# A two-block transformer kernel: the feed-forward up and gate products streamed as 512 columns into a whole PSUM bank

## The chip, the core and the metric

One core of a Trainium2 chip runs the whole program as one launch. The engines of a core are TensorE (PE; its weight loads are listed as PEld), VectorE (DVE), ScalarE (ACT), GpSimd (POOL) and SyncE (SP, which here only issues loads of weights). Matrix products accumulate in PSUM, which has eight banks of 512 fp32 columns on 128 partitions. The metric is the device time of the kernel in microseconds (us), as the median of several runs; less is better.

## The reference

The input is 256 rows (tokens) of 1024 numbers. Two transformer blocks follow one another. What matters here are their three feed-forward parts, one in the first block and two in the second:

```
# first block
a, v = split(h @ w_up)                    # h = rmsnorm(x), 1024 -> 2 x 2816
a    = causal depthwise conv, 3 taps, + bias
x    = x + (gelu(a) * v) @ w_down         # 2816 -> 1024
# second block, before and after its attention
x    = x + 0.5 * ((silu(h @ w_gate) * (h @ w_up)) @ w_down)
```

All inputs and outputs are fp32, and each product is computed to about fp32 accuracy.

## The kernel before

**Products.** TensorE reads fp32 here in a faster, rounded format (F32R). So every operand is split into a high half (the rounded value, made by ACT) and a low half (the rest, made by DVE), and a product is three matmuls: high x high, high x low, low x high, added up in PSUM. The helper `three` (line 336) does it for each block of 128 contracted numbers.

**Units.** Weights come in 158 units, nearly all of 1 MB, in the order of a plan. For unit i, SP loads `raw[i % 3]`, ACT copies it to `wh[i % 3]` (line 880), DVE subtracts and writes `wl[i % 3]` (line 1292). `hi_to(i)` and `lo_to(i)` make the halves up to unit i; `begin(key, ahead=2)` makes them up to two units past `key`. ACT's copy waits until the products of unit i - 3 are done, SP's load until `wl` of unit i - 3 is made. Each engine runs its own program strictly in the order in which it is written; semaphores tie them together.

**A feed-forward part** `ffn(f, k, ...)` (f = 0, 1, 2; k numbers the norm ahead of it) runs over 11 steps j. Step j has two up units, ("up", f, j, 0), here called the a unit, and ("up", f, j, 1), the v unit. Each gives 256 columns of the inner width, turned so that they lie on partitions (two groups m of 128), for 256 tokens: 2 groups x 8 blocks k x 3 matmuls of 256 tokens, 48 matmuls, into one bank (`rows_out`). Then comes the down unit of step j - 1 with 24 matmuls of 512 columns, whose sums stay in banks 2 to 5. The turned rows of h stand in `hTh` and `hTl`, 256 columns for each block. DVE takes a unit out of its bank and multiplies by `RB`, the norm's factor for each token (`rows_scaled`, line 1376). ACT applies silu (for f = 0: three taps, ACT's on line 1165, DVE's on line 1842, and gelu on line 1168), DVE multiplies a and v (line 1851), ACT and DVE split the result into `yTh` (line 1182) and `yTl` (line 1862), and only then does each of them make its halves of one more weight unit.

**The start of a part.** Step j = 0 runs its two units as a pair (`norm_pair`), in four stretches of 24 matmuls: blocks 4 to 7 of a, then of v, then blocks 0 to 3 of a, then of v, because blocks 0 to 3 of h come last. Eight transposes (line 385) stand after the first stretch and a small product (line 399), which spreads the token factors, after the third. A pair takes four banks, one for each unit and group m, and its factors are applied by `pair_scaled` (line 1367). At this place ACT makes `wh` of the two units that follow the pair.

**Banks.** Up units take turns on banks 0, 1, 6, 7 (`WF`); the projections ahead of a part use banks 0 and 1 (`W`); transposes and spreads use 2 to 5. A unit's first matmul waits until the engine that emptied the bank before has counted it free (`take`).

Of the kernel before, what the change touches and what calls it, by code (L numbers as in the profile page):

```python
# [123 lines left out]
def build(nc, plan, I, out):  # L124
    ctx = ExitStack()
    with ctx:
# [9 lines left out]
        wl = [sb(f"wl{i}", 2048, F32R) for i in range(NS)]  # L136
        hTh, hTl = sb("hTh", 2048, F32R), sb("hTl", 2048, F32R)
        X, Hn = sb("X", 2048), sb("Hn", 2048)
# [13 lines left out]
        F2 = sb("F2", 256)  # L152
        bank = [ctx.enter_context(nc.psum_tensor(f"ps{i}", [128, 512], F32)) for i in range(8)]

# [48 lines left out]
        mrg_fox, mrg_all, m_hi, m_lo = (sem(n) for n in ("mrg_fox", "mrg_all", "m_hi", "m_lo"))  # L203

        cv_in, cv_out, ff_act, ff_y, y_hi, y_lo = (sem(n) for n in ("cv_in", "cv_out", "ff_act", "ff_y", "y_hi", "y_lo"))

# [71 lines left out]
        def hT_at(k):  # L278
            return hTh[:, k * 256:k * 256 + 256], hTl[:, k * 256:k * 256 + 256]

        def yT_at(k):
            return yTh[:, k * 256:k * 256 + 256], yTl[:, k * 256:k * 256 + 256]
# [34 lines left out]
        def pe_program(pe):  # L317
            W, T = Banks(0, 1), Banks(2, 3, 4, 5)
            WF = Banks(0, 1, 6, 7)

# [9 lines left out]
            def three(o, lw, rw, ks, first, last, ready=None):  # L330
                (lh, ll), (rh, rl) = lw, rw
                for k in ks:
                    for j, (l, r) in enumerate(((lh, rh), (lh, rl), (ll, rh))):
                        if j == 0 and ready is not None and (k == ks[0] or k % 2 == 0):
                            pe.wait_ge(*ready(k))
                        ins = pe.matmul(o, l(k), r(k), start=first and k == ks[0] and j == 0,  # L336
                                        stop=last and k == ks[-1] and j == 2)
                return ins

# [14 lines left out]
            def rows_out(key, banks, mid=None):  # L354
# [3 lines left out]
                for m in range(2):  # L358
                    ins = three(t[:, m * 256:m * 256 + 256], weight_left(i, 256, m * 128), right(hT_at),
                                EIGHT, True, True)  # L360
                    if m == 0 and mid:
                        mid()
                ins.then_inc(ps_full[b], 1)
                unit_end[i] = full(key)
# [38 lines left out]
            def norm_pair(key0, key1, k):  # L403
                keys = (key0, key1)
                bs = [[WF.take(), WF.take()] for _ in range(2)]
                for half, ks in enumerate(((4, 5, 6, 7), (0, 1, 2, 3))):
                    for j in range(2):
# [13 lines left out]
                        if half:  # L421
                            unit_end[i] = full(keys[j] + (1,))
                        if half and j == 0:
                            spread(k)
# [323 lines left out]
            def ffn(f, k, k_next):  # L748
                for j in range(11):
                    if j == 0:  # L750
                        norm_pair(("up", f, 0, 0), ("up", f, 0, 1), k)
                    else:
                        rows_out(("up", f, j, 0), WF)
                        rows_out(("up", f, j, 1), WF)
                    if 1 <= j < (9 if k_next is None else 10):
# [23 lines left out]
            def last_units(f):  # L779
# [14 lines left out]
                unit_end[U["down", f, 9]] = full(("acc", f, 1))  # L794

                for h in range(2):
                    b = WF.take()
                    t = take(("last", h), b)
# [4 lines left out]


            norm_pair(("qa", 0), ("ka", 0), 3)
            toks_out(("va", 0), W)
# [61 lines left out]
        def act_program(act):  # L868
# [49 lines left out]
            def norm_turns(k, hold):  # L918
                act.wait_ge(*x_ready(k, 0))
                act.wait_ge(*x_ready(k, 1))  # L920
                squares(k, 0)
                if hold is not None:
                    act.wait_ge(*unit_end[hold])
                for p in (0, 1):
# [220 lines left out]
            def toeplitz():  # L1145
# [136 lines left out]
        def dve_program(dve):  # L1282
# [537 lines left out]
            def ffn(f, k, scale, k_next):  # L1820
                for j in range(11):
# [4 lines left out]
                    if j == 0:  # L1826
                        norm_pair(ka, k)
                        pair_scaled(g, ka)
                        pair_scaled(gv, kv)
                        lo_to(U[ka] + 3)  # L1830
                    else:
                        begin(ka)
                        rows_scaled(g[:, :], ka)
                        begin(kv)
# [11 lines left out]
                    if j:  # L1846
                        rows_scaled(gv[:, :], kv)
                        dve.wait_ge(*free(kv))
                    else:
                        dve.wait_ge(*free(kv + (1,)))  # L1850
                    dve.tensor_tensor(g[:, :], gv[:, :], c[:, :], ALU.mult).then_inc(ff_y, 1)  # L1851
# [377 lines left out]
```

## Time and profile before

| what | value |
|---|---|
| median of 3 runs | 1000.81 us (1000.48 to 1001.31) |
| profiled execution, its own time | 1000.7 us |
| span of its trace | 998.9 us |
| PE busy | 985.7 us, 99% |
| weight loads busy | 944.4 us, 95% |
| DVE busy | 665.8 us, 67% |
| ACT busy | 487.1 us, 49% |
| POOL busy | 69.0 us, 7% |
| weights and inputs read | 172.21 MB, 173 GB/s over the span |

A busy time is the union of an engine's instructions. Matmuls overlap one another: a record of one is 0.28 us long, but one starts every 0.12 us. So what a matmul costs is read from the distance between starts, or from a long piece of the chain divided by its count, and not from its own duration. For DVE and ACT the duration is nearly the cost; the next independent instruction starts 0.05 to 0.1 us before the end of the one ahead.

### The profile page before, as it was taken

What the parts mean: (1) busy time and instruction counts of PE and PEld (TensorE: products, weight loads), DVE (VectorE), ACT (ScalarE), POOL (GpSimd) and SP (SyncE); (2) the same over time, 40 slices, a digit from 0 to 9 for tenths busy, and PEclk for the clock granted to TensorE, in tenths of its full rate; (3) what the DMA queues carried; (4) which work ended last, traced back from release to release, by engine and by line L of the source; (5) the groups of instructions that cost most, each with busy time, mean ns of one, the idle gap of its engine ahead of it and who ended that gap; (6) DMA issues with size and microseconds to landing.
All of it is one profiled execution on the core that took longest, in us unless ns stands there. A gap on an engine that the chain in (4) does not pass through costs nothing.

```text
span 998.9 us, 17282 instructions
## 1 busy us (share of the span) xinstructions
PE 985.7 (99%) x7438; PEld 944.4 (95%) x7438; DVE 665.8 (67%) x849; ACT 487.1 (49%) x588; POOL 69.0 (7%) x148
## 2 busy tenths in 40 slices
PE   7999999999999999999999999999999999999997
PEld 7999999999999999999899999999999999999996
DVE  5679767775776766676675555557777576555565
ACT  6654656565355545444554333336545453333343
POOL 0010123234210000000000000000002000000000
PEclk9999999999999999999999999999999999999999
DMA  9744444343455555454456455553533445555541
GB/s 337 279 133 163 135 161 170 132 152 140 138 206 210 211 189 191 172 200 156 174 185 208 172 183 197 171 192 134 179 131 123 142 174 212 183 197 171 192 144 43
DMA packets 26539, 174.37 MB, mean 175 GB/s; under 512 B 3424, under 2 KB 3808, under 8 KB 6368
## 3 DMA queue, kind: packets, MB, share of 16 engines
q1 hardware_dynamic: 25744, 170.23, 48.0%
q10 hardware_dynamic: 720, 3.04, 0.8%
q8 instruction: 59, 0.97, 0.4%
q14 instruction: 16, 0.13, 0.0%
HBM read 172.21 MB, written 1.05 MB: 173 GB/s over the span
## 4 chain that ended last, share of the span: by engine, by line
PE 98%; DVE 0%; ACT 0%; DMA 0%; issue 0%; ACTq 0%
PE ps L336 90%; PE ps L570 2%; PE ps L621 2%; PE ps L385 1%; PE ps L489 1%; PE ps L584 1%; DMA GT<-in_gains 0%; PE ps L399 0%; PE ps L479 0%; PE ps L514 0%; DVE hTl L1321 0%; ACT hTh L894 0%; ACT hTh L916 0%; PE ps L513 0%; PE ps L497 0%
## 5 line engine op out<-in xcount | busy, mean ns | idle before, releaser
L336 PE MATMUL ps<-hTh,wh 128*128 128x256 f32 x1512 | 432.4, 286 | 6.8 <-DVE wl L1407 6.5
L336 PE MATMUL ps<-hTh,wl 128*128 128x256 f32 x1512 | 428.7, 284 | 0.0
L336 PE MATMUL ps<-hTl,wh 128*128 128x256 f32 x1512 | 428.6, 283 | 0.0
L1292 DVE TENSOR_TENSOR wl<-raw,wh 128x2048 fp32r<-128x2048 f32 x153 | 350.7, 2293 | 109.4 <-ACT wh L880 109.3
L880 ACT ACTIVATE wh<-raw 128x2048 fp32r<-128x2048 f32 x156 | 295.6, 1899 | 177.3 <-PE ps L336 173.1
L336 PEld LDWEIGHTS ps<-hTh,wh 128*128 128x128 f32 x1512 | 290.1, 192 | 9.5 <-DVE wl L1407 6.5
L336 PEld LDWEIGHTS ps<-hTl,wh 128*128 128x128 f32 x1512 | 290.0, 192 | 1.4
L336 PEld LDWEIGHTS ps<-hTh,wl 128*128 128x128 f32 x1512 | 290.0, 192 | 0.2
L336 PE MATMUL ps<-wh,yTh 128*128 128x512 f32 (+1 forms) x330 | 123.3, 374 | 0.0
L336 PE MATMUL ps<-wl,yTh 128*128 128x512 f32 (+1 forms) x330 | 122.9, 373 | 0.0
L336 PE MATMUL ps<-wh,yTl 128*128 128x512 f32 (+1 forms) x330 | 122.8, 372 | 0.0
L336 PE MATMUL ps<-wh,hTh 128*128 128x256 f32 x384 | 110.8, 289 | 0.0
L336 PE MATMUL ps<-wh,hTl 128*128 128x256 f32 x384 | 108.5, 283 | 0.0
L336 PE MATMUL ps<-wl,hTh 128*128 128x256 f32 x384 | 108.5, 283 | 0.0
L1376 DVE TENSOR_TENSOR PT<-ps,RB 128x512 f32<-128x512 f32 x60 | 41.4, 691 | 74.2 <-PE ps L336 67.2
L1182 ACT ACTIVATE yTh<-PT 128x512 fp32r<-128x512 f32 x33 | 20.9, 634 | 110.9 <-DVE PT L1851 107.1
L336 PEld LDWEIGHTS ps<-wl,hTh 128*128 128x128 f32 x384 | 73.6, 192 | 0.1
L336 PEld LDWEIGHTS ps<-wh,hTh 128*128 128x128 f32 x384 | 73.4, 191 | 0.1
L336 PEld LDWEIGHTS ps<-wh,hTl 128*128 128x128 f32 x384 | 73.5, 191 | 0.0
L336 PEld LDWEIGHTS ps<-wh,yTl 128*128 128x128 f32 x330 | 62.1, 188 | 11.9
L336 PEld LDWEIGHTS ps<-wh,yTh 128*128 128x128 f32 x330 | 62.3, 189 | 10.6
L336 PEld LDWEIGHTS ps<-wl,yTh 128*128 128x128 f32 x330 | 62.2, 188 | 10.6
(250 smaller groups left out, 791.6 us busy)
## 6 DMA issues: line engine op xcount, KB each, us to landing
raw<-in_units SPq DMA_DIRECT2D x155, 1024.0 KB, 4.9
BIGT<-in_bias ACTq DMA_DIRECT2D x1, 2048.0 KB, 7.5
XT<-in_x_turned SPq DMA_DIRECT2D x4, 256.0 KB, 5.4
raw<-in_units SPq DMA_DIRECT2D x4, 256.0 KB, 5.6
raw<-in_units SPq DMA_DIRECT2D x2, 512.0 KB, 8.2
X<-in_x SPq DMA_DIRECT2D x1, 1024.0 KB, 8.5
Hn<-in_mem SPq DMA_DIRECT2D x1, 1024.0 KB, 10.0
XT<-in_mem_turned SPq DMA_DIRECT2D x1, 1024.0 KB, 12.1
```

The source lines that it names most:

```text
L336: ins = pe.matmul(o, l(k), r(k), start=first and k == ks[0] and j == 0, stop=last and k == ks[-1] and j == 2)
L385: ins = pe.transpose(t[:, q * 128:q * 128 + 128], src[:, m * n + k * 128:m * n + k * 128 + 128], ident)
L489: ins = pe.matmul(t[:, q * 128:q * 128 + 128], s, s, start=True, stop=True)
L570: ins = pe.matmul(t[:, x:z], l, r, start=True, stop=True)
L584: ins = pe.transpose(t[:, j * 128:j * 128 + 128], src[:, o:o + 128], ident)
L621: ins = pe.matmul(at_o(m), turned(a, i)[:, j * 128:j * 128 + 128], at_v(kb), start=x == 0, stop=x == len(js) - 1)
L880: act.activation(wh[j % NS][:, 0:n], raw[j % NR][:, 0:n], ACT.Copy).then_inc(w_hi, 1)
L1182: act.activation(yTh[:, j % 2 * 512:j % 2 * 512 + 512], g[:, :], ACT.Copy).then_inc(y_hi, 1)
L1292: dve.tensor_tensor(wl[j % NS][:, 0:n], raw[j % NR][:, 0:n], wh[j % NS][:, 0:n].bitcast(F32), ALU.subtract).then_inc(w_lo, 1)
L1376: ins = dve.tensor_tensor(o, i, by_token(2), ALU.mult)
```

## The change

The two halves of h become one tensor `hT`, with `hTh` and `hTl` as its two parts, and the eight banks become one tensor `ps`. For the up units alone, a new helper `crossed` runs two matmuls instead of three for each block and group: the high weights against both halves of h at once (512 columns, read as two pieces of 256 which lie 2048 columns apart), then the low weights against the high half (256 columns, added to the second half of the bank). A unit then fills two whole banks, one for each group m, and the result is the sum of a bank's two halves. ACT copies the second halves out of PSUM into `Am` (`second_sums`), DVE adds them to the first halves (`up_scaled`, first instruction) and then multiplies by `RB` (second instruction). Up units take turns on two pairs of banks, (0, 1) and (6, 7). The counters of `W` and `WF` are set back to zero after the second part.

```diff
+        def hT_both(k):
+            return hT[:, :].rearrange("p (s n) -> p s n", s=2)[:, :, k * 256:k * 256 + 256]
...
+            def crossed(o, lw, ks, first, last, ready=None):
+                lh, ll = lw
+                for k in ks:
...
+                    pe.matmul(o, lh(k), hT_both(k), start=first and k == ks[0], stop=False)
+                    ins = pe.matmul(o[:, 256:512], ll(k), hT_at(k)[0], start=False, stop=last and k == ks[-1])
+                return ins
...
-            WF = Banks(0, 1, 6, 7)
+            WF, UP = Banks(0, 1, 6, 7), Banks(0, 6)
...
+            def take_two(key):
+                b = UP.take()
+                return b, [take(key, b), take(key + ("x",), b + 1, False)]
...
# ACT
+            def second_sums(key):
+                n, (_, t) = up_no(key), sums(key)
+                act.wait_ge(*full(key))
+                if n >= 2:
+                    act.wait_ge(*free(up_key(n - 2)))
+                act.activation(v3(crossed_out(n)), t, ACT.Copy).then_inc(cross_made, 1)
...
                     if j == 0:
-                        norm_pair(keys[0], k)
+                        hi_to(U[keys[0]] + 1)
+                        norm_turns(k, U["wo", k, 1] if k == 1 or k == 4 else U["up", k - 2, 10, 1])
+                        second_sums(keys[0])
+                        hi_to(U[keys[0]] + 3)
                     else:
                         begin(keys[0])
+                        second_sums(keys[0])
                         begin(keys[1])
-                    act.wait_ge(*free(keys[0] if j else keys[0] + (1,)))
+                    act.wait_ge(*scaled(keys[0]))
...
+                    if not j:
+                        second_sums(keys[1])
...
+                    if j:
+                        second_sums(keys[1])
...
# DVE
+            def up_scaled(dst, key):
+                n, d, (t, _) = up_no(key), v3(dst), sums(key)
+                dve.wait_ge(cross_made, n + 1)
+                dve.tensor_tensor(d, t, v3(crossed_out(n)), ALU.add).then_inc(*emptied(key))
+                dve.wait_ge(*free(key))
+                dve.tensor_tensor(d, d, by_token(2), ALU.mult).then_inc(*emptied(key + ("x",)))
...
-                        pair_scaled(g, ka)
-                        pair_scaled(gv, kv)
+                        up_scaled(g[:, :], ka)
+                        up_scaled(gv[:, :], kv)
                         lo_to(U[ka] + 3)
...
+            W.n, WF.n = 0, 0
             norm_pair(("qa", 0), ("ka", 0), 3)
```

How the programs stand at three places follows. Names in the rows: `ps_full` counts filled banks, `ps_free` emptied ones, the digit is the bank.

ACT at the start of the second part, before, from the last block of h (`hTh`) on: the two copies `wh` are those of the a and v units of step 1.

```order
L894 ACTIVATE hTh<-ps4,GT 128x256 [waits ps_full4,ps_full0]
L894 ACTIVATE hTh<-ps4,GT 128x256
L894 ACTIVATE hTh<-ps5,GT 128x256 [waits ps_full5]
L894 ACTIVATE hTh<-ps5,GT 128x256
L880 ACTIVATE wh0<-raw0 128x2048 [waits raw_in0,ps_full5]
L880 ACTIVATE wh1<-raw1 128x2048 [waits raw_in1,ps_full6]
L1174 ACT_TABLE_LOAD
L1174 ACTIVATE P0<-PT0 128x512 [waits ps_free6]
```

The same place with the change:

```order
L963 ACTIVATE hT<-ps,GT 128x256
L963 ACTIVATE hT<-ps,GT 128x256 [waits ps_full5]
L963 ACTIVATE hT<-ps,GT 128x256
L1225 ACTIVATE Am<-ps 128x512 [waits ps_free0,ps_full0]
L949 ACTIVATE wh0<-raw0 128x2048 [waits raw_in0,ps_full5]
L949 ACTIVATE wh1<-raw1 128x2048 [waits raw_in1,ps_full0]
L1225 ACTIVATE Am<-ps 128x512 [waits ps_free6,ps_full6,ps_free1]
L1256 ACT_TABLE_LOAD
L1256 ACTIVATE P0<-PT0 128x512
```

A copy out of PSUM that waits for the a unit of the pair (`ps_full0`) now stands ahead of both `wh` copies; before, only the second of them waited for that unit.

PE at the start of the first part, before: the last matmuls of the projection's last unit, which fills bank 0, and the first two of the pair.

```order
L336 MATMUL ps<-wh,hTh 128x256
L336 MATMUL ps<-wl,hTh 128x256
L336 MATMUL ps<-wh,hTl 128x256
L336 MATMUL ps<-hTh,wh 128x256 [waits ps_free3,w_lo,ps_free1]
L336 MATMUL ps<-hTl,wh 128x256
```

The same place with the change, where the projection's last unit fills bank 0 as well:

```order
L360 MATMUL ps<-wh,hT 128x256 x2
L360 MATMUL ps<-wl,hT 128x256
L360 MATMUL ps<-wh,hT 128x256
L370 MATMUL ps<-hT,wh 128x512 [waits w_lo,ps_free3,ps_free1,ps_free0]
L371 MATMUL ps<-hT,wl 128x256
```

The pair's first matmul waited for bank 1; it now waits for banks 0 and 1, and bank 0 is the one that the unit just ahead of it has filled. At the start of the third part the last projection fills bank 1, and it is bank 1 that is new in the wait. 
PE at the start of the first part, before: the end of the pair and the first matmuls of the unit after it.

```order
L336 MATMUL ps<-hTh,wh 128x256
L336 MATMUL ps<-hTl,wh 128x256
L336 MATMUL ps<-hTh,wl 128x256
L336 MATMUL ps<-hTh,wh 128x256 [waits w_lo,ps_free1]
L336 MATMUL ps<-hTl,wh 128x256
```

The same place with the change:

```order
L370 MATMUL ps<-hT,wh 128x512
L371 MATMUL ps<-hT,wl 128x256
L370 MATMUL ps<-hT,wh 128x512 [waits w_lo,ps_free1,ps_free0]
L371 MATMUL ps<-hT,wl 128x256
L370 MATMUL ps<-hT,wh 128x512
```

The unit after a pair now waits for two banks. Bank 0 counts as free after DVE's addition for the pair's a unit, bank 1 after the multiplication behind it. Before, this matmul waited for one bank alone, which one instruction of `pair_scaled` empties.

## Rows read from the trace of the kernel before

**Rows 1.** The page: busy time by engine, and the chain by engine and line.

```profile
PE 985.7 (99%) x7438; PEld 944.4 (95%) x7438; DVE 665.8 (67%) x849; ACT 487.1 (49%) x588; POOL 69.0 (7%) x148
PE 98%; DVE 0%; ACT 0%; DMA 0%; issue 0%; ACTq 0%
```

**Rows 2.** The chain in order of time: start, length, work, count.

```profile
497.84 5.75 PE ps L336 x48
...
769.05 1.29 PE ps L621 x12
...
813.01 179.76 PE ps L336 x1254
```

**Rows 3.** PE in order of time: start, length of record. First part, the pair's first matmul.

```profile
303.01 0.28 PE L336 MATMUL ps<-hTh,wh 128*128 128x256 f32 x1
```

**Rows 4.** DVE in order of time: the addition that empties the projection's last bank.

```profile
303.21 0.69 DVE L1810 TENSOR_TENSOR X<-X,ps 128x512 f32<-128x512 f32 x1 [0.38 <-PE ps L336]
```

**Rows 5.** DVE, then PE: a wait of PE that ends, second part's start.

```profile
492.83 1.66 DVE L1321 SCALAR_TENSOR_TENSOR hTl<-ps,GT,hTh 128x256 fp32r<-128x256 f32 x4 [0.35 <-ACT hTh L894]
493.86 0.35 PE L336 MATMUL ps<-hTh,wh 128*128 128x256 f32 x1 [0.15 <-DVE hTl L1321]
```

**Rows 6.** ACT in order of time, second part's start; then a PSUM copy elsewhere.

```profile
498.94 1.93 ACT L880 ACTIVATE wh<-raw 128x2048 fp32r<-128x2048 f32 x1
503.63 1.92 ACT L880 ACTIVATE wh<-raw 128x2048 fp32r<-128x2048 f32 x1 [2.76 <-PE ps L336]
...
140.54 0.60 ACT L1024 ACTIVATE P<-ps 128x512 f32<-128x512 f32 x1 [1.19 <-PE ps L514]
141.03 1.91 ACT L880 ACTIVATE wh<-raw 128x2048 fp32r<-128x2048 f32 x1
```

**Rows 7.** DVE in order of time, second part's start.

```profile
502.50 2.28 DVE L1292 TENSOR_TENSOR wl<-raw,wh 128x2048 fp32r<-128x2048 f32 x1
504.70 0.42 DVE L1351 COPY RB<-ps 128x256 f32<-128x256 f32 x1
505.15 0.76 DVE L1367 TENSOR_TENSOR PT<-ps,RB 128x256 f32<-128x256 f32 x2
```

**Rows 8.** PE in order of time: the first matmul of the unit after the pair.

```profile
506.75 0.28 PE L336 MATMUL ps<-hTh,wh 128*128 128x256 f32 x1
```

**Rows 9.** ACT in order of time, first part, step 1.

```profile
331.40 0.63 ACT L1168 ACTIVATE P<-P 128x512 f32<-128x512 f32 x1 [2.81 <-DVE P L1842]
333.52 0.63 ACT L1182 ACTIVATE yTh<-PT 128x512 fp32r<-128x512 f32 x1 [1.48 <-DVE PT L1851]
334.05 3.70 ACT L880 ACTIVATE wh<-raw 128x2048 fp32r<-128x2048 f32 x2
```

**Rows 10.** DVE in order of time, first part, step 1.

```profile
326.79 0.68 DVE L1376 TENSOR_TENSOR PT<-ps,RB 128x512 f32<-128x512 f32 x1
327.39 2.28 DVE L1292 TENSOR_TENSOR wl<-raw,wh 128x2048 fp32r<-128x2048 f32 x1
329.58 1.78 DVE L1842 SCALAR_TENSOR_TENSOR P<-PT,VT,P 128x255 f32<-128x255 f32 x4
332.07 0.69 DVE L1376 TENSOR_TENSOR PT<-ps,RB 128x512 f32<-128x512 f32 x1 [0.70 <-ACT P L1168]
332.79 0.69 DVE L1851 TENSOR_TENSOR PT<-PT,P 128x512 f32<-128x512 f32 x1
335.99 4.49 DVE L1292 TENSOR_TENSOR wl<-raw,wh 128x2048 fp32r<-128x2048 f32 x2 [1.11 <-ACT wh L880]
```

**Rows 11.** Stretches: start:end, their length, PE, PEld, DVE, ACT, POOL busy, PEclk.

```profile
6.50:11.70 5.20, 5.19 (x24) 5.19 (x25) 3.99 (x9) 4.39 (x9) 0.00 (x0) 1.00 0.98 347
992.00:993.00 1.00, 0.76 (x7) 0.55 (x5) 0.70 (x3) 0.38 (x2) 0.00 (x0) 1.00 0.99 371
994.50:995.00 0.50, 0.00 (x0) 0.00 (x0) 0.43 (x3) 0.07 (x1) 0.00 (x0) 0.77 0.00 0
995.00:995.50 0.50, 0.00 (x0) 0.00 (x0) 0.50 (x1) 0.50 (x1) 0.00 (x0) 0.50 0.00 0
```

More of the change, by code:

```diff
@@ L136, in build @@
         wl = [sb(f"wl{i}", 2048, F32R) for i in range(NS)]
-        hTh, hTl = sb("hTh", 2048, F32R), sb("hTl", 2048, F32R)
+        hT = sb("hT", 4096, F32R)
+        hTh, hTl = hT[:, 0:2048], hT[:, 2048:4096]
         X, Hn = sb("X", 2048), sb("Hn", 2048)
@@ L152, in build @@
         F2 = sb("F2", 256)
-        bank = [ctx.enter_context(nc.psum_tensor(f"ps{i}", [128, 512], F32)) for i in range(8)]
+        ps = ctx.enter_context(nc.psum_tensor("ps", [128, 4096], F32))
+        bank = [ps[:, 512 * i:512 * i + 512] for i in range(8)]
         used = [0]
@@ L279, in hT_at, with sums, scaled, up_no @@
             return hTh[:, k * 256:k * 256 + 256], hTl[:, k * 256:k * 256 + 256]
+        def hT_both(k):
+            return hT[:, :].rearrange("p (s n) -> p s n", s=2)[:, :, k * 256:k * 256 + 256]
+        def sums(key):
+            t = ps[:, 512 * at[key][0]:512 * at[key][0] + 1024].rearrange("p (m s n) -> p m s n", m=2, s=2)
+            return t[:, :, 0, :], t[:, :, 1, :]
+        def scaled(key):
+            return free(key + ("x",))
+        def up_no(key):
+            return 22 * key[1] + 2 * key[2] + key[3]
+        def up_key(n):
+            return "up", n // 22, n // 2 % 11, n % 2
+        def crossed_out(n):
+            return Am[:, n % 2 * 512:n % 2 * 512 + 512]
         def yT_at(k):
@@ L337, in three @@
                                         stop=last and k == ks[-1] and j == 2)
+                return ins
+            def crossed(o, lw, ks, first, last, ready=None):
+                lh, ll = lw
+                for k in ks:
+                    if ready is not None and (k == ks[0] or k % 2 == 0):
+                        pe.wait_ge(*ready(k))
+                    pe.matmul(o, lh(k), hT_both(k), start=first and k == ks[0], stop=False)
+                    ins = pe.matmul(o[:, 256:512], ll(k), hT_at(k)[0], start=False, stop=last and k == ks[-1])
                 return ins
@@ L362, in rows_out, with up_out @@
                         mid()
+                ins.then_inc(ps_full[b], 1)
+                unit_end[i] = full(key)
+            def take_two(key):
+                b = UP.take()
+                return b, [take(key, b), take(key + ("x",), b + 1, False)]
+            def up_out(key):
+                i = U[key]
+                b, ts = take_two(key)
+                weights(i)
+                for m in range(2):
+                    ins = crossed(ts[m], weight_left(i, 256, m * 128), EIGHT, True, True)
                 ins.then_inc(ps_full[b], 1)
@@ L422, in norm_pair, with up_pair @@
                             unit_end[i] = full(keys[j] + (1,))
+                        if half and j == 0:
+                            spread(k)
+            def up_pair(key0, key1, k):
+                keys, bs, ts = (key0, key1), [0, 0], [None, None]
+                for half, ks in enumerate(((4, 5, 6, 7), (0, 1, 2, 3))):
+                    for j in range(2):
+                        i = U[keys[j]]
+                        if not half:
+                            bs[j], ts[j] = take_two(keys[j])
+                            weights(i)
+                        for m in range(2):
+                            ins = crossed(ts[j][m], weight_left(i, 256, m * 128), ks, half == 0, half == 1,
+                                          (lambda k2: free(("n", k, k2 // 2))) if j == 0 and m == 0 else None)
+                        if half:
+                            ins.then_inc(ps_full[bs[j]], 1)
+                            unit_end[i] = full(keys[j])
+                        if not half and j == 0:
+                            norm_turn(k, 0)
+                            norm_turn(k, 1)
                         if half and j == 0:
@@ L750, in ffn @@
                     if j == 0:
-                        norm_pair(("up", f, 0, 0), ("up", f, 0, 1), k)
+                        up_pair(("up", f, 0, 0), ("up", f, 0, 1), k)
                     else:
-                        rows_out(("up", f, j, 0), WF)
-                        rows_out(("up", f, j, 1), WF)
+                        up_out(("up", f, j, 0))
+                        up_out(("up", f, j, 1))
                     if 1 <= j < (9 if k_next is None else 10):
@@ L794, in last_units @@
                 unit_end[U["down", f, 9]] = full(("acc", f, 1))
+                b0 = UP.take()
                 for h in range(2):
-                    b = WF.take()
+                    b = b0 + h
                     t = take(("last", h), b)
@@ L1832, in ffn @@
                         begin(ka)
-                        rows_scaled(g[:, :], ka)
+                        up_scaled(g[:, :], ka)
                         begin(kv)
@@ L1846, in ffn @@
                     if j:
[L1847 to L1850, printed above, removed]
+                        up_scaled(gv[:, :], kv)
+                    dve.wait_ge(*scaled(kv))
                     dve.tensor_tensor(g[:, :], gv[:, :], c[:, :], ALU.mult).then_inc(ff_y, 1)
```

4 lines of the change are left out of this document (2 added, 2 removed).

## The prediction

> **What bounds the kernel now.** I read the page first: PE is busy 99% of the span, and 98% of the chain that ended last is PE work [rows 1]. The chain in order of time then shows the feed-forward parts as single pieces, 1254 matmuls in 179.76 us in the third one, with no wait inside [rows 2]. So each ns of a matmul counts in full, and so does each ns that PE waits; DVE (67%) and ACT (49%) [rows 1] have room, on average. What they add costs nothing in the middle of a part unless a chain of their steps gets longer than PE's step, and it may cost at once where PE waits for their latest result. That place is the start of each part, so I read all engines there in order of time [rows 3 to 8].
>
> **What a matmul costs.** 48 matmuls of 256 columns take 5.75 us, 119.8 ns each [rows 2]. Of the 1254 in the third part, 996 have 256 columns; they leave 179.76 - 996 x 0.1198 = 60.4 us for 258 matmuls of 512, 234.3 ns each. Three of 256 cost 359.4 ns, one of 512 and one of 256 cost 354.1 ns: the same 768 columns pass, and only one start is saved. **The gain is 5.3 ns** for each block and group, 0.085 us a unit. There are 66 units x 16 = 1056 of them: **-5.6 us** in all.
> Bounds: if a 256 costs half a 512 (117.1 ns) once it stands behind one, the gain is 8.0 ns or 8.4 us. On the other side, no row shows an operand read as two pieces 2048 columns apart; if the second piece costs as much as a new start, the 512 costs 2 x 119.8 and the gain is nil. I take 5.3 ns, since the streamed columns are the same kind of F32R data as in both rows.
> The Trainium skill (TensorE: Matmul & The Clock Gate, Back-to-back issue gap) gives N/2.4 + 2.5 ns at the full clock, which would make one saved start worth 2.5 ns, an estimate of 2.6 us for the change. The rows are above it at both widths.
>
> **A new wait ahead of the first and the third pair.** The pair's first matmul starts at 303.01 [rows 3], right behind the projection's last unit. DVE empties that unit's bank from 303.21 to 303.90 [rows 4]. The pair will now ask for that bank. When a wait of PE ends, its matmul starts 0.14 us behind the releasing work (DVE's first two of four pieces end near 493.72, PE starts at 493.86), and its record is 0.07 us longer [rows 5]. So it starts at 303.90 + 0.14 + 0.07 = 304.11: 1.1 us late, twice, **+2.2 us**. The second part comes behind units that use other banks and doesn't pay.
>
> **A new wait behind each pair.** Second part, with times of before. ACT copied the high half of the unit behind the pair (P2) at 498.94, long before it was needed, and that of P3 at 503.63, when the pair's a unit was done [rows 6]. Now a copy out of PSUM that waits for the a unit stands ahead of both.
> - The a unit is done after three stretches, 0.04 us sooner each: 503.50. The PSUM copy holds ACT 0.49 us (140.54 to 141.03) [rows 6]. P2's high half starts at 503.99.
> - DVE subtracts 1.94 us later (334.05 to 335.99) [rows 9, 10]: at 505.93, instead of 502.50 [rows 7].
> - DVE's next steps keep their distances: `RB` 2.20 later at 508.13, the addition 0.45 later at 508.58 [rows 7], the multiplication, which needs its result, 0.72 later at 509.30 (332.07 to 332.79), done after 0.69 at 509.99 [rows 10].
> - P2 needs both banks of the a unit. It starts at 509.99 + 0.21 = 510.20. It started at 506.75 [rows 8], and with four shorter stretches would at 506.58. **The wait is 3.6 us**: DVE's work on the bank begins 3.4 us later (508.58 for 505.15 [rows 7]), and takes 1.4 us for both banks where one piece of some 0.4 was enough; 0.8 us of room is used up.
> Three parts: **+10.9 us**. The spread and the low half of the pair's factors have no part in it; they were ready at 502.50.
>
> **The first part has two more.** There the three taps make DVE's and ACT's chain longer. Let M be the end of the multiplication above; P2 starts at M + 0.2, P3 at M + 5.9, the first down unit should at M + 11.5. The chain: PSUM copy for v and its addition (M + 0.65), multiplication (+0.72), low half of P3 (+0.60), taps (+2.20), gelu (+1.82), a x v (+0.67), `yTh` (+0.73), high half of the down unit (+0.53), its low half (+1.94) for 2.29 us [rows 9, 10]: ends at M + 12.15, and PE goes on at M + 12.4. **+0.8 us.**
> One step on: additions from M + 12.06, low half 13.4, taps 15.6, gelu 17.4, then in turn PSUM copy, addition, multiplication, a x v, `yTh`, high half, 5.8 us together, and the low half of the next v unit from M + 23.2 to 25.5. PE, coming from M + 12.4 + 5.6 + 5.7 = M + 23.7, goes on at M + 25.7. **+2.1 us.** After that the chain's round (three low halves 6.6, addition and multiplication 1.3, taps 1.8, gelu 0.5, PSUM copy 0.6, addition to `yTh` 2.9, high half 1.9) is 15.6 us, 16.6 where ACT also turns a bias (1.05 us), against PE's 32 x 0.354 + 24 x 0.234 = 17.0. It catches up slowly. At the part's end the same chain from the last a unit is 11.2 us against PE's 11.3, which with the restart is worth **+0.2**. In the other parts there are no taps (2 us less), and nothing of this waits.
>
> **The sum.** -5.6 + 2.2 + 10.9 + 0.8 + 2.1 + 0.2 = +10.6 us, on the profiled execution's own 1000.7 us (span 998.9 and 1.8 around it; the median is 1000.81): 1011.3.
>
> **The clock.** PE was busy 99% [rows 1] and after its start the chain holds no wait as long as these. At the end PE's last work ends at 992.76, and the granted clock falls to half (1.2 GHz) near 994.77 (0.77 over that half us), 2.0 us later [rows 11]. A wait of 3.6 us is longer. At the kernel's start 24 matmuls took 5.19 us, where 24 x 0.12 = 2.9 is full speed [rows 11, 2], though the record there reads 1.00; that is half speed (1.2 GHz) after idling: 2.3 us is the most that one fall costs, nothing the least. I take the middle, 1.1, since the fall may come before or after the restart, for the second and third part: **+2.2 us**. In the first part the later waits are timed by ACT and DVE and swallow it.
> The Trainium skill says the same of idling (same page, What's actually happening: the default is the half rate and activity releases it). **1013.5 us.**
>
> **Rivals.**
> - The clock stays up: 1011.3. For it: one fall is all that the trace shows.
> - The two-piece operand eats the gain: 1013.5 + 5.6 = 1019.1. Against: nothing; no row shows one.
> - The waits of the first part are smaller (a hop or two shorter, since they hang on the sum of ten steps) and the clock stays up: 1000.7 - 5.6 + 2.2 + 10.9 = 1008.2.
> - Faster. What spaces the 256-column matmuls is the weight load, and the one behind a 512 finds its weights loaded and costs 256/2.4 = 106.7 ns. The pair is then 341.0 ns, the gain 18.4 ns x 1056 = 19.4 us: 1000.7 - 19.4 + 16.2 = 997.5. It is faster from a gain of 15.3 ns each on. Against: 512 columns take 234.3, so columns cost more than 1/2.4 ns; and matmuls of 64 columns, each with a load, come every 107 ns (12 in 1.29 us) [rows 2], so a load doesn't need 119.8.
>
> **How the numbers follow.** The forecast 40% (own range 1011 to 1016), clock up 27%, smaller first part 13%, gain eaten 12%, faster mechanism 8%, of which a part lands within 0.2%. 0.2% (2 us) is about what a measurement of this kernel can tell from no change. The range 1007 to 1018 holds the first three cases. Faster 0.06, same 0.04, slower 0.90.
>
> **What would show it.** In the chain, between the piece of a pair and the long piece behind it, a DVE multiplication into `PT` as PE's releaser, some 3.6 us after the pair; ACT's `Am` copy at the pair's third stretch and P2's `wh` behind it; a wait of 1.1 us ahead of the first and third pair, released by DVE's addition into `X`; two waits of PE on `wl` in the first part's steps 1 and 2, none in the others; a long piece of the third part of about 178 us; a granted clock below 1 in the 5 us behind P2's start. I am wrong if P2 starts on time, or if the matmul pair is far from 354 ns.

## The result, and the profile after

| | before | after |
|---|---|---|
| median | 1000.98 us (1000.48 to 1001.31, 4 runs) | 1011.11 us (1008.4 to 1012.12, 4 runs) |
| profiled execution | 1000.7 us | 1011.95 us |
| span of its trace | 998.9 us | 1010.1 us |

The ratio after to before is 1.0099, with a 95% interval of 1.0083 to 1.0116: the change costs 1%. From the page after: busy time by engine, then the chain by engine, then the two new instructions (busy time, mean ns | idle time before and what ended it):

```profile
PE 983.3 (97%) x6382; PEld 892.5 (88%) x6382; DVE 708.6 (70%) x909; ACT 521.2 (52%) x654; POOL 68.8 (7%) x148
...
PE 91%; DVE 4%; ACT 2%; issue 1%; POOL 1%; DMA 0%; ACTq 0%; DVEq 0%
...
L1225 ACT ACTIVATE Am<-ps 128x512 f32<-128x512 f32 x66 | 39.3, 596 | 152.6 <-PE ps L371 145.6
L1460 DVE TENSOR_TENSOR PT<-ps,Am 128x512 f32<-128x512 f32 x66 | 45.6, 691 | 84.4 <-ACT Am L1225 84.3
```

Against [rows 1]: 1056 matmuls fewer, as the diff says. ACT has 34 us more work and DVE 43, and neither is the bound: ACT is busy 52% and DVE 70%. But PE's share of the chain fell from 98% to 91%, so other engines now stand in the path. The view that names the places is that of PE's waits (what PE waited for: us in all, times, the longest). Its head after:

```profile
PE ps L370 <- DVE PT L1462: 10.3, 3, 3.4
PE ps L360 <- DVE wl L1499: 6.5, 1, 6.5
PE ps L370 <- DVE wl L1376: 1.5, 1, 1.5
PE ps L370 <- issue: 0.8, 1, 0.8
PE ps L370 <- DVE X L1902: 0.8, 1, 0.8
PE ps L360 <- DVE yTl L1952: 0.2, 1, 0.2
```

and before, at the head of the same view:

```profile
PE ps L336 <- DVE wl L1407: 6.5, 1, 6.5
PE ps L336 <- DVE hTl L1321: 0.3, 2, 0.2
```

The 6.5 us is in both, at the kernel's start. New are three waits on the multiplication into `PT` that frees the pair's second bank, two ahead of the first and the third pair (the view gives the addition into `X` for one and no releaser, `issue`, for the other; there the same addition ended at 811.90 and PE started at 812.00), and one of 1.5 us on a low half `wl`.

The start of the second part after the change, ACT, DVE and PE merged in order of time (start, length, then the idle time before and who ended it), to be read against [rows 6 to 8]:

```profile
508.62 0.60 ACT L1225 ACTIVATE Am<-ps 128x512 f32<-128x512 f32 x1 [4.46 <-PE ps L371]
509.12 3.71 ACT L949 ACTIVATE wh<-raw 128x2048 fp32r<-128x2048 f32 x2
511.06 2.29 DVE L1376 TENSOR_TENSOR wl<-raw,wh 128x2048 fp32r<-128x2048 f32 x1 [3.38 <-ACT wh L949]
513.27 0.42 DVE L1435 COPY RB<-ps 128x256 f32<-128x256 f32 x1
513.72 0.69 DVE L1460 TENSOR_TENSOR PT<-ps,Am 128x512 f32<-128x512 f32 x1
514.45 0.69 DVE L1462 TENSOR_TENSOR PT<-PT,RB 128x512 f32<-128x512 f32 x1
515.24 0.76 PE L370 MATMUL ps<-hT,wh 128*128 128x512 f32 x1 [3.43 <-DVE PT L1462]
```

ACT was idle for 4.46 us ahead of `Am`, with P2's weights in place and waiting to be copied behind it (in the first experiment below ACT copies them at 502.30). Then each hop follows the one ahead: 0.50 for the copy out of PSUM, 1.94 for `wh`, 2.21 for `wl`, 0.45 for `RB`, 0.73 for the addition, 0.79 from the multiplication to PE. These are the prediction's hops to within 0.02 us, but for the last, which was forecast at 0.90.

And the granted clock at that place (stretch start:end, length, busy PE, PEld, DVE, ACT, POOL, then PEclk):

```profile
512.00:514.00 2.00, 0.00 (x0) 0.00 (x0) 1.97 (x3) 0.83 (x1) 0.00 (x0) 1.00 0.00 0
514.00:516.00 2.00, 0.76 (x2) 0.69 (x3) 1.30 (x3) 0.81 (x2) 0.00 (x0) 0.52 0.85 242
516.00:518.00 2.00, 2.00 (x9) 1.71 (x8) 1.97 (x3) 1.71 (x2) 0.00 (x0) 0.50 0.67 283
518.00:520.00 2.00, 2.00 (x8) 1.71 (x8) 2.00 (x2) 0.00 (x0) 0.00 (x0) 0.50 0.00 0
520.00:522.00 2.00, 2.00 (x11) 1.67 (x10) 0.72 (x2) 1.94 (x2) 0.00 (x0) 0.77 0.78 188
```

PE did nothing from 511.8 on, the clock fell to half (1.2 GHz) near 514, and it stayed there until 521, 5.8 us into PE's new work, which began at 515.24. One matmul of 512 and one of 256 columns then take 0.64 us together instead of 0.35.

**Where the 11.2 us of span are.** PE's own time line divides the kernel into blocks that can be set side by side. A pair block here runs from the last twelve matmuls ahead of the pair (in the second part, from the pair itself) to the first down unit, so it holds the pair, P2 and P3. Stretches of before: the pair block of the first part, the first part's last down unit, the second part's pair block, a steady stretch of two up units, and the third part's pair block.

```profile
301.57:327.35 25.78, 25.78 (x219) 25.78 (x217) 17.84 (x34) 13.87 (x17) 0.00 (x0) 1.00 0.48 174
...
481.43:491.26 9.83, 9.83 (x44) 7.87 (x43) 6.57 (x8) 6.19 (x7) 0.00 (x0) 1.00 0.39 136
493.86:518.27 24.41, 24.41 (x204) 24.41 (x205) 18.81 (x33) 13.42 (x16) 0.00 (x0) 1.00 0.45 153
541.01:552.51 11.50, 11.50 (x97) 11.50 (x96) 6.14 (x4) 4.35 (x3) 0.00 (x0) 1.00 0.56 188
801.47:827.25 25.78, 25.78 (x219) 25.78 (x217) 18.40 (x31) 13.42 (x16) 0.00 (x0) 1.00 0.46 155
```

The same after. The second row has the v unit's late start in step 2, a stretch that took 11.51 us before; the fifth and the sixth are two steady stretches.

```profile
301.38:332.72 31.34, 27.14 (x154) 23.54 (x153) 19.33 (x34) 15.32 (x20) 0.00 (x0) 0.95 0.38 142
338.33:351.31 12.98, 11.45 (x66) 9.79 (x65) 10.80 (x10) 7.78 (x8) 0.00 (x0) 1.00 0.48 177
485.84:496.37 10.53, 10.23 (x44) 7.65 (x43) 7.36 (x11) 5.98 (x7) 0.00 (x0) 1.00 0.36 111
499.02:529.02 30.00, 26.57 (x140) 22.99 (x141) 20.93 (x34) 15.09 (x19) 0.00 (x0) 0.89 0.42 142
534.63:545.92 11.29, 11.29 (x65) 9.80 (x64) 8.12 (x5) 4.84 (x4) 0.00 (x0) 1.00 0.50 186
551.54:562.65 11.11, 11.11 (x66) 9.79 (x65) 8.13 (x5) 4.85 (x4) 0.00 (x0) 1.00 0.53 190
809.57:841.10 31.53, 27.28 (x154) 23.65 (x153) 20.21 (x32) 15.10 (x19) 0.00 (x0) 0.95 0.39 130
```

The three pair blocks cost 5.56, 5.59 and 5.75 us more. The end of the first part costs 0.70. All other up stretches (25 of two units, step 2 of the first part among them, and a last one of four) give 6.4 us back, the 1.8 us of step 2 already taken off. 16.9 + 0.7 - 6.4 = 11.2. So nothing is lost outside these places. Down units take 5.62 us in both kernels.

### The profile page after: what moved, and what is told of

Read it like the earlier page. It is cut to its first block, busy times and chain, and to the rows that moved or that the text cites. A ratio compares the mean times of both kernels' runs of the same rounds, so it can differ in the third digit from the quotient of the medians.

```text
span 1010.1 us, 15364 instructions
## 1 busy us (share of the span) xinstructions
PE 983.3 (97%) x6382; PEld 892.5 (88%) x6382; DVE 708.6 (70%) x909; ACT 521.2 (52%) x654; POOL 68.8 (7%) x148
## 4 chain that ended last, share of the span: by engine, by line
PE 91%; DVE 4%; ACT 2%; issue 1%; POOL 1%; DMA 0%; ACTq 0%; DVEq 0%
PE ps L360 49%; PE ps L370 23%; PE ps L371 12%; PE ps L637 2%; PE ps L688 2%; DVE wl L1376 2%; PE ps L432 1%; PE ps L556 1%; ACT wh L949 1%; PE ps L651 1%; DVE PT L1462 0%; DVE PT L1460 0%; DVE P L1934 0%; DMA GT<-in_gains 0%; POOL sm L2113 0%
## 5 line engine op out<-in xcount | busy, mean ns | idle before, releaser
L370 PE MATMUL ps<-hT,wh 128*128 128x512 f32 x1056 | 378.0, 401 | 13.6 <-DVE PT L1462 10.3
L371 PE MATMUL ps<-hT,wl 128*128 128x256 f32 x1056 | 298.3, 283 | 0.0
L370 PEld LDWEIGHTS ps<-hT,wh 128*128 128x128 f32 x1056 | 200.7, 190 | 62.9 <-DVE PT L1460 11.1
L371 PEld LDWEIGHTS ps<-hT,wl 128*128 128x128 f32 x1056 | 202.1, 191 | 1.1
L360 PE MATMUL ps<-hT,wh 128*128 128x256 f32 (+1 forms) x912 | 170.8, 289 | 6.7 <-DVE wl L1499 6.5
L360 PEld LDWEIGHTS ps<-hT,wh 128*128 128x128 f32 (+1 forms) x912 | 143.1, 192 | 7.8 <-DVE wl L1499 6.5
L360 PE MATMUL ps<-wh,hT 128*128 128x256 f32 x768 | 146.3, 286 | 0.0
L360 PE MATMUL ps<-hT,wl 128*128 128x256 f32 (+1 forms) x456 | 130.1, 285 | 0.0
L360 PEld LDWEIGHTS ps<-wh,hT 128*128 128x128 f32 x768 | 122.1, 191 | 0.1
L360 PE MATMUL ps<-wl,hT 128*128 128x256 f32 x384 | 108.5, 283 | 0.0
## 6 DMA issues: line engine op xcount, KB each, us to landing
Hn<-in_mem SPq DMA_DIRECT2D x1, 1024.0 KB, 10.9
```

What stands on the lines that cost most here:

```text
L370: pe.matmul(o, lh(k), hT_both(k), start=first and k == ks[0], stop=False)
L371: ins = pe.matmul(o[:, 256:512], ll(k), hT_at(k)[0], start=False, stop=last and k == ks[-1])
```

## The experiments

Two theories stand against each other on the main loss. The first: it comes from order alone; ACT's `Am` copy waits for the pair's a unit with P2's `wh` behind it. The second: it comes from what the change adds (two banks to free, two more instructions a unit), so it stays wherever the copy stands. The other open points are the size of the gain, the two-piece operand, and the clock.

### The high half ahead of the copy, with the change

```diff
                         norm_turns(k, U["wo", k, 1] if k == 1 or k == 4 else U["up", k - 2, 10, 1])
+                        hi_to(U[keys[0]] + 2)
                         second_sums(keys[0])
                         hi_to(U[keys[0]] + 3)
```

> The changed kernel with one line more: at the start of a part ACT makes the high half of the unit behind the pair (P2) before it waits for the pair's a unit, as the kernel before did. Theory: this removes the waits of 3.4 us behind the three pairs all but 0.2 us each, and with them the falls of the clock; the 1.5 us ahead of the first and third pair and the waits inside the first part (0.8 and 2.1 us, no longer hidden by the slow clock) stay. 1000.7 - 7.0 (matmuls, at 6.6 ns a pair as the changed kernel's trace has it) + 1.5 + 0.6 + 2.9 + 0.2 = 998.9 us, granted clock 1.00 behind the pairs. Rival: the time goes to the added copies, additions and multiplications themselves, and the place of one copy hardly matters: 1008 to 1011 us.

Measured: 999.07 us (997.23 to 1002.59, 10 runs), ratio to before 0.9985 (0.9972 to 0.9998). One copy is moved, and the time is 12.0 us below that of the change as made, which had lost 10.1. No wait on `PT` is left in the view of PE's waits. Behind the 6.6 us of the kernel's start it has:

```profile
PE ps L370 <- DVE wl L1377: 2.0, 1, 2.0
PE ps L360 <- DVE wl L1377: 1.0, 1, 1.0
PE ps L370 <- issue: 0.8, 1, 0.8
PE ps L370 <- DVE X L1903: 0.8, 1, 0.8
```

The second theory falls: the two banks and the added instructions are still there. DVE's multiplication now starts at 509.24 in the second part, and P2 doesn't wait for it. What stands first now are the first part's two waits on low halves, 2.0 and 1.0 us where the changed kernel had 1.5 and none: what came before them no longer delays PE.

The runs of this kernel lie further apart than those of any other here. They sort by the mean granted clock: 0.998 or 0.999 for those of 997.2 to 997.7 us, 0.997 for 998.7 to 1000.5, 0.995 for the two above 1001. The expected 998.9 us was met in part by luck: it took the matmuls' gain at 7.0 us, where 9.1 were measured (see the last experiment), and no fall of the clock. The profiled run shows a fall behind the wait of 2.0 us, which ended at 342.34:

```profile
340.00:342.00 2.00, 0.37 (x3) 0.05 (x1) 2.00 (x1) 2.00 (x2) 0.00 (x0) 1.00 0.00 0
342.00:344.00 2.00, 1.66 (x7) 1.51 (x8) 2.00 (x2) 1.95 (x2) 0.00 (x0) 0.76 0.37 66
344.00:346.00 2.00, 2.00 (x8) 1.71 (x7) 1.97 (x4) 0.24 (x1) 0.00 (x0) 0.50 0.95 397
```

### The late high half alone, without the change

The other way round: the kernel before, with the wait for the pair's a unit put ahead of both `wh` copies, and nothing else.

```diff
                 norm_turns(k, U["wo", k, 1] if k in (1, 4) else U["up", k - 2, 10, 1])
+                if k != 3:
+                    act.wait_ge(*unit_end[U[key]])
                 hi_to(U[key] + 3)
```

> The kernel before with one wait more: at the start of each part ACT waits for the pair's a unit before it makes the high half of P2. Nothing else is changed, no fused matmul, no added copy, one bank a unit. Theory: the a unit is done at 503.63 in the second part, P2's low half starts 1.94 later, the token factors 2.20 on, the bank of the pair's first group is empty at 508.64, and PE starts P2 at 508.85 instead of 506.75: 2.1 us a part, 6.3 in all, 1007 us, and up to 1.5 us more in a part where the clock falls, which a wait of 2 us may or may not bring about: 1007 to 1010. Rival: the order on ACT is harmless by itself and only hurts with the added additions: 1001.

Measured: 1008.17 us (1007.65 to 1010.23), ratio 1.0075 (1.0059 to 1.009). So a wait that has nothing to do with the fused products costs the kernel before 7.5 us by itself. Its waits on `PT`, then four stretches from the second and the third part:

```profile
PE ps L336 <- DVE PT L1369: 5.4, 3, 1.8
...
513.00:515.00 2.00, 2.00 (x15) 2.00 (x14) 2.00 (x3) 0.57 (x1) 0.00 (x0) 0.72 0.71 270
515.00:517.00 2.00, 2.00 (x12) 2.00 (x11) 1.37 (x2) 0.59 (x2) 0.00 (x0) 0.50 0.85 254
...
824.00:826.00 2.00, 0.84 (x7) 0.84 (x8) 1.97 (x6) 1.62 (x2) 0.00 (x0) 1.00 0.40 57
826.00:828.00 2.00, 2.00 (x19) 2.00 (x18) 2.00 (x2) 0.10 (x1) 0.00 (x0) 1.00 0.86 356
```

Here a clean price of the clock can be read. The same wait of 1.8 us stands in all three parts. In the first and the second the clock fell behind it, and the blocks from the pair to the first down unit are 3.54 and 3.57 us longer than before (29.32 for 25.78, 27.98 for 24.41). In the third it stayed up, and the block is 2.06 longer (27.84 for 25.78). One fall costs 1.5 us here, and the same wait need not bring it. In the second part PE started again at 512.63 and the clock fell near 513.9, behind the restart, and came back near 517.3.

### Work for PE in the wait

27 products of 256 columns, whose result nobody reads, stand behind each pair, 3.2 us at 119.8 ns each. They fill the wait on `PT` without changing when it ends.

```diff
                     if j == 0:
                         up_pair(("up", f, 0, 0), ("up", f, 0, 1), k)
+                        for _ in range(27):
+                            pe.matmul(bank[at["n", k, 1][0]][:, 0:256], hT_at(0)[0][:, 0:128], hT_at(0)[0], start=True, stop=True)
```

> The changed kernel with 27 more matmuls of 256 columns (3.2 us) behind each pair, into a bank that nobody reads, where PE would wait 3.4 us. P2 can start no earlier or later for them. Theory: the wait stays, but the granted clock no longer falls; the second part wins back 8.7 matmul pairs x 0.29 = 2.5 us and the third 1.4 us, the first part little, since its next wait on a low half takes it back: 1007 to 1008 us, and the same in every run within 1 us, where the changed kernel's runs spread over 4 us. Rival: the slow clock is no part of the loss: 1011 us.

Measured: 1007.41 us (1006.55 to 1008.89), ratio 1.0071 (1.0056 to 1.0086): 3.7 us less than the changed kernel, with 81 products more. The stretches of the second part's start:

```profile
512.00:514.00 2.00, 2.00 (x19) 2.00 (x18) 1.97 (x3) 0.80 (x1) 0.00 (x0) 1.00 0.00 0
514.00:516.00 2.00, 1.86 (x14) 1.60 (x14) 1.30 (x3) 0.84 (x2) 0.00 (x0) 1.00 0.83 205
```

The clock stays at 1.00, and P2 starts at 515.21, as before at 515.24. From one part's `RB` copy to the next (for the last, to the end of the span), the second part takes 187.86 us instead of 190.48 and the third 181.96 instead of 183.82. So the falls cost 2.6 and 1.9 us there. The first part takes 195.14 instead of 195.21: nothing is won, because two waits on low halves, 2.1 and 0.6 us, take the place of the fall and of the 1.5 us. The prediction said of this part that ACT's and DVE's chain swallows the clock, and this run shows it. One thing expected did not come: the runs lie 2.3 us apart, not within 1, and the slowest shows a mean granted clock of 0.997 for the profiled one's 0.999.

### How much the fused matmul is worth

In this kernel the high weights go against the two halves in two matmuls again, except for the first block of each group, which still fills the whole bank. 7/8 of the change's gain is taken away, and all its order is kept.

```diff
-                    pe.matmul(o, lh(k), hT_both(k), start=first and k == ks[0], stop=False)
+                    if first and k == ks[0]:
+                        pe.matmul(o, lh(k), hT_both(k), start=True, stop=False)
+                    else:
+                        for s in range(2):
+                            pe.matmul(o[:, 256 * s:256 * s + 256], lh(k), hT_at(k)[s], start=False, stop=False)
```

> The changed kernel, but the high weights meet the two halves of h in two matmuls of 256 columns instead of one of 512, except for the first block of each group; banks, copies, additions and all waits as changed. It prices the fused matmul alone. Theory: 7 of 8 of 1056 x 6.6 ns come back, +6 us, a part of it hidden in the first part's waits: 1015 to 1017 us. Rival: the operand in two pieces costs as much as a second start and the fused matmul gives nothing: no difference, 1011 us.

Measured: 1020.05 us (1019.96 to 1020.14), ratio 1.0195 (1.0178 to 1.0212). That is 8.9 us more than the changed kernel, where 7/8 of the predicted 5.6 would be 4.9, and above the expected 1015 to 1017. Over 924 blocks it is 9.7 ns each. The clock doesn't explain it: PE worked at half clock for 12.4 us in this trace and for 11.9 in the changed kernel's, a difference worth some 0.3 us. A steady stretch of two up units takes 11.49 us, where it took 11.50 before, so the second bank, the copies and the additions cost nothing there:

```profile
570.65:582.14 11.49, 11.49 (x94) 11.30 (x92) 8.12 (x5) 4.83 (x4) 0.00 (x0) 1.00 0.49 184
```

### The operand in one piece

The 512 columns are read from one place without a gap in all units outside the pairs. The address is the only difference (they are then the wrong columns, so the kernel serves for its time alone).

```diff
+                rb = (lambda k: hT[:, k * 512:k * 512 + 512]) if first and last else hT_both
...
-                    pe.matmul(o, lh(k), hT_both(k), start=first and k == ks[0], stop=False)
+                    pe.matmul(o, lh(k), rb(k), start=first and k == ks[0], stop=False)
```

> The changed kernel, but in all up units outside the pairs the 512 columns are read as one contiguous piece instead of two pieces 2048 columns apart (so they are not the right columns and the output is not the reference's; all else is as changed). Theory: the two pieces cost nothing, the distance of a 512 to its 256 stays 0.234 us and the time 1011 us. Rival: the second piece costs a start of about 5 ns, and 960 of them come back: 1006 us and 0.229 us.

Measured: 1011.04 us (1010.34 to 1011.96), ratio 1.0106 (1.0091 to 1.0121), against 1011.11 with two pieces. Its steady stretches:

```profile
550.20:561.30 11.10, 11.10 (x65) 9.78 (x64) 8.11 (x5) 4.84 (x4) 0.00 (x0) 1.00 0.51 190
566.92:578.21 11.29, 11.29 (x65) 9.80 (x64) 8.12 (x5) 4.84 (x4) 0.00 (x0) 1.00 0.50 186
```

The second piece costs nothing. The prediction's rival in which it eats the gain (1019.1 us) falls. The lengths of 11.1 and 11.3 us that take turns are not from the pieces either.

### The first banks taken in the other order

With the high half moved ahead as in the first experiment, the up units also begin with banks 6 and 7 instead of 0 and 1, so that the first and the third pair don't ask for the bank that the projection has just filled.

```diff
-            WF, UP = Banks(0, 1, 6, 7), Banks(0, 6)
+            WF, UP = Banks(0, 1, 6, 7), Banks(6, 0)
```

> The changed kernel with the early high half of the first experiment, and with the turns of the up units' banks the other way round, (6, 7) first, so that the pair no longer asks for the bank that the projection ahead of it has just filled. Theory: against the first experiment (999.1) the waits of 0.8 us ahead of the first and third pair go: 997.5. The waits inside the first part and the clock's fall behind them stay, with their spread of some us between runs. Rival: the banks cost nothing, the pair would wait for something else: 999.

Measured: 997.53 us (996.93 to 999.34, 5 runs), ratio 0.9972 (0.996 to 0.9984), where 997.5 was expected. Its waits in the first part:

```profile
PE ps L370 <- DVE wl L1377: 2.0, 1, 2.0
PE ps L360 <- DVE wl L1377: 0.8, 1, 0.8
```

Both waits ahead of the pairs are gone. From the start of the first part's pair block to the transposes behind the pair's first stretch PE takes 4.28 us, where it took 5.31 in the first experiment. That is 1.03 us for a wait that its row gave as 0.8: idle time is counted from the end of a record, and records of matmuls run 0.16 us longer than their distance, while the first one behind a wait has 0.1 us more.

### The first part's chain, one step and two steps

What is left is ACT's and DVE's chain in the first part. On top of the two edits before, the high and the low half of one unit more are made as soon as the taps and the a x v product are issued, in step 0 only.

```diff
 # ACT, behind its taps
+                        if j == 0:
+                            hi_to(U[keys[0]] + 4)
                         act.wait_ge(cv_out, 2 * j + 2)
 # DVE, behind a x v
                     dve.tensor_tensor(g[:, :], gv[:, :], c[:, :], ALU.mult).then_inc(ff_y, 1)
+                    if f == 0 and j == 0:
+                        lo_to(U[ka] + 4)
```

> The kernel of the run before, and in step 0 of the first part the halves of the first down unit are made earlier: ACT's while DVE works on the taps, DVE's right behind the product a x v, ahead of yTl. Theory: the waits of 1.0 and 2.0 us inside the first part go, and with them the clock's fall there. What is left is the gain of the fused matmuls, 9.4 ns x 1056 = 9.9 us as the up stretches of the changed kernel have it (11.20 us instead of 11.50), less 0.5 us of small waits: 1000.7 - 9.9 + 0.5 = 991.3, and runs within 0.5 us of one another. Rival: the first part is bound by the chain on DVE and ACT, round after round, and the wait only moves to a later step: 995 to 997.

Measured: 994.20 us (992.73 to 994.53, 5 runs), ratio 0.9932 (0.992 to 0.9945). It lies between the two cases, 991.3 and 995 to 997: the down unit's wait is gone, but the v unit's in step 2, which was to go as well, went only from 2.0 to 1.2 us.

```profile
PE ps L370 <- DVE wl L1379: 1.2, 1, 1.2
```

The same in steps 0 and 1 (`j < 2` in both places):

> As the run before (994.2 us), with the halves of the unit made early in step 1 of the first part too, as in step 0. There the run before still had one wait of 1.2 us, at the v unit of step 2. Theory: DVE's subtraction starts 2.6 us sooner (right behind the product, not behind yTh and a high half), the wait goes, and 1.2 to 1.7 us with it: 992.5 to 993.0. Rival: the chain on DVE and ACT is a bound of the first part, and the wait moves one step on again: 994.

Measured: 991.79 us (991.65 to 992.23, 4 runs), against 1000.42 (1000.03 to 1001.54) for the kernel before on the same chip, ratio 0.9912 (0.9896 to 0.9929). That is below the expected 992.5 to 993.0. No wait on a low half is left in the parts. The first 45 us of the first part, then its three pair blocks:

```profile
300.00:345.00 45.00, 45.00 (x259) 39.10 (x258) 36.91 (x53) 25.88 (x34) 0.00 (x0) 1.00 0.58 209
...
301.10:326.61 25.51, 25.51 (x154) 22.35 (x153) 19.49 (x35) 15.34 (x20) 0.00 (x0) 1.00 0.49 177
491.04:515.00 23.96, 23.95 (x140) 20.89 (x141) 18.68 (x34) 14.43 (x19) 0.00 (x0) 1.00 0.42 138
795.56:821.07 25.51, 25.51 (x154) 22.36 (x153) 18.43 (x32) 14.59 (x19) 0.00 (x0) 1.00 0.42 138
```

PE is busy throughout at the full clock, and the runs lie within 0.6 us of one another, where those of the change as made spread over 3.7. This version is faster than both kernels. The traces (span 990.1 us for 998.9) say where the gain is. The up stretches outside the pair blocks give 8.1 us back, 9.4 ns a block. The pair blocks, which hold no wait and no fall now, give only 0.27, 0.45 and 0.27 back, where 9.4 ns for each of their 64 blocks would be 0.60. So the fused matmuls are worth 9.1 us in the whole kernel. The end of the first part still costs 0.7, and the stretch up to the first part was 0.5 shorter in this run, in the first projections, which no edit touches.

## Why the prediction was right, and where its steps were off

The time, 1011.11 us, lies in the range, 2.4 below the forecast. The sign and the mechanism held. By its terms, for the profiled execution:

| term | predicted | measured |
|---|---|---|
| fused matmuls, 1056 | -5.6 | -9.1 |
| wait ahead of the first and third pair | +2.2 | +2.1 |
| wait behind the three pairs | +10.9 | +11.1 |
| first part: down unit of step 1 | +0.8 | 0 |
| first part: v unit of step 2 | +2.1 | +1.8 |
| first part: its end | +0.2 | +0.7 |
| the clock | +2.2 | +4.7 |
| sum | +12.8 | +11.3 |

The execution was 11.25 us longer. That the forecast came within 2.4 us is in part luck: the gain was 3.5 us larger than said and the clock 2.5 us dearer, and the two errors cancel for the most part. The measured waits are the idle times of the rows (3.4, 0.8 and 1.5) with the 0.26 us added that the bank experiment showed a row to leave out. The gain and the clock are measured against the last experiment's blocks.

- **The wait behind the pairs** is the step that decides, and it was right in place, cause and size: 3.7 us each for 3.6. The first experiment takes it away by order alone, and the late high half alone brings it into the kernel before (1.8 us there; that it is shorter since no second bank and no addition stand behind it was only argued).
- **The wait ahead of the first and the third pair** came as said, at 303.76 and again at 812.00, 1.0 us each. Taking the banks in the other order removed it.
- **The fused matmuls** are the step that failed. The prediction took 354.1 ns a pair from the rows of 256 and 512 columns apart, and bounded the gain at 8.4 us from above. The steady stretches give (11.29 + 11.11) / 2 / 32 = 350.0 ns, for 359.4: 9.4 ns a block, and 9.1 us in the whole kernel, since the pair blocks gain less. Starts in the rows of a long and a short stretch lie 236 and 230 ns apart from a 512 to its 256, and 117 ns from the 256 to the next 512. So the 256 costs behind a 512 what the prediction's bound gave it (117.1) and not what it costs among its own kind (119.8), and in the short stretches the 512 is below its 234.3 as well. The value was taken from matmuls among their own kind, and the bound let only the 256 differ, so it was too narrow. The Trainium skill (TensorE: Matmul & The Clock Gate, Back-to-back issue gap) would have a saved start worth 2.5 ns, an estimate of 2.6 us for the change; the rows give three and a half times that.
- **The clock** is the second one. It fell in all three parts. Set against the pair blocks of the last experiment, and with both waits taken off, the blocks are 1.1, 2.4 and 1.3 us too long (some 18 pairs of matmuls ran at half speed, each 0.29 us longer, which gives as much to within 0.2). The run with work in the wait says 2.6 and 1.9 for the second and third part. The prediction halved what one fall may cost, 1.1, because it might come before or after the restart. In this trace it came before the restart each time. And a fall that came 1.2 us behind it, in the kernel with the late high half alone, cost 1.5 all the same, so the moment of the fall was no ground to halve. Twice the whole 2.3 us, 4.6, would have been nearer to the 3.7 and 4.5 us that the two ways of reading give for these two parts.
- **The first part**: the fall's 1.1 us stands in the place of the down unit's 0.8. PE came late enough for its low half. With the clock up there (in the first experiment and in the one with work in the wait) the wait is there, 1.0 and 0.6 us. So the chain of ten steps was worked out rightly, and only its price changed hands. At the part's end the chain cost 0.5 us more than said: PE waits for `yTl` at 491.86, and it starts the transposes 0.2 us late.
- **The rivals**: that the clock stays up ended at 1011.3, nearest to the result, but by errors that cancel: 3.5 us more gain, and 4.7 us of a clock that it put at nothing. Its condition did not hold. The smaller first part did not come: 2.5 us of the 3.1. The faster mechanism (997.5) had the right direction for the distance of two matmuls, but 18.4 ns where 9.4 were measured; to be faster the change would have needed 15.3 ns a block.

Not settled: why the steady stretches take 11.29 and 11.11 us by turns. It isn't the operand's pieces and not the order at the pair, since the one-piece kernel and that of the first experiment have it too. The banks and the weight buffers are the same in every step, and the a unit in banks 0 and 1 takes as long as the v unit in 6 and 7 (5.64 and 5.65 us in a long stretch, 5.56 and 5.55 in a short one). It isn't the step's number either: step 2 is long in the second part and short in the third.

## What to carry to other kernels

When an edit makes an engine wait for a result, list what is queued behind that wait on the same engine, at the starts of parts first. There a copy that was ready early became late, and a change that gained 8.6 us in the best order tried lost 10.1; one moved copy took 12.0 us back. The PE waits of 1.8 to 3.4 us here cost themselves and, where the clock fell, 1.1 to 2.6 us more behind them, so count both. Where runs of one kernel spread, sort them by their mean granted clock: in the first experiment that explained the spread. Spread alone is no sign of such a wait; two of 13 runs of the kernel before took 1003.1 and 1003.5 us with a mean clock no lower than the others. And the price of a matmul among its own kind is not its price beside another kind, so let both prices differ when you bound the gain of fusing two.

## What the runs showed of the hardware beyond that

- A matmul of 512 and one of 256 F32R columns by turns take 347 to 353 ns together, where 119.8 and 234.3 ns are their distances among their own kind, so the pair is 1 to 7 ns shorter than their sum.
- An operand of 512 columns in two pieces 2048 columns apart runs as fast as one in a single piece (1011.11 and 1011.04 us).
- The same wait of 1.8 us let PE's clock fall in two of its three places. Behind a wait PE can run at half clock for some microseconds while it is busy throughout: in the changed kernel to 521 for work that began at 515.24.
- 81 products that nobody needs made the kernel 3.7 us faster: where the changed kernel's stretches show a granted clock of 0.50, this kernel's profiled run shows 1.00.
